# A fused hybrid-mixer and ConvFFN layer on one core: two early steps of the up stage moved, the residual loads of the down stage split up, and the last scaling shared by two engines

## What is computed

```python
h = rmsnorm(x, norm1_g)
x = x + hybrid_mixer(h, ...)          # attention and mLSTM heads, W_in and W_out
h = rmsnorm(x, norm2_g)
u = causal_dwconv(h @ w_up, w_conv, b_conv)      # w_up 1024 x 5632, three taps
gate, up = split(u, 2)
x = x + (silu(gate) * up) @ w_down               # w_down 2816 x 1024
return rmsnorm(x, final_g)
```

## Time and profile before

| | |
|---|---|
| median of 3 runs | 1053.67 us (1052.75 to 1054.21) |
| profiled execution: its own time | 1054.37 us |
| its span, first to last instruction | 1052.6 us |
| PE busy | 1024.2 us (97% of the span) |
| DVE busy | 728.0 us (69%) |
| ACT busy | 500.2 us (48%) |
| mean granted PE clock | 0.994 of full speed |
| DMA | 107.75 MB, mean 102 GB/s |
| raw<-in_w_up, 512 KB: median from issue to landing | 4.8 us |

### The profile page before, as it was taken

The page is one execution under the profiler, slowest core; times in us unless marked ns, Lnnn a source line. Parts: engine busy times, 40 slices in busy tenths (PEclk is TensorE's granted clock), DMA queues, the critical chain, the costliest instruction groups (busy, mean ns, idle before and its releaser), DMA issues.

```text
span 1052.6 us, 13256 instructions
## 1 busy us (share of the span) xinstructions
PE 1024.2 (97%) x4933; PEld 845.9 (80%) x4933; DVE 728.0 (69%) x1153; ACT 500.2 (48%) x939; POOL 74.4 (7%) x80
## 2 busy tenths in 40 slices
PE   5999999999989999799999999999999999999997
PEld 4888888888778888688888888888888887888886
DVE  5352555641675567898778777777787778996796
ACT  7632445443653324465445445454454634444564
POOL 5020222220330000000000000000000000000000
PEclk9999999999999999899999999999999999999999
DMA  7126111110242224233223122231230998125104
GB/s 223 43 73 149 40 31 30 40 41 21 62 140 81 80 80 140 60 101 115 66 81 100 60 94 88 80 100 60 81 101 21 362 391 306 59 86 186 58 1 161
DMA packets 108640, 107.75 MB, mean 102 GB/s; under 512 B 13330, under 2 KB 81032, under 8 KB 108576
## 3 DMA queue, kind: packets, MB, share of 16 engines
q1 hardware_dynamic: 107040, 103.56, 31.1%
q0 software_dynamic: 1536, 3.34, 1.3%
HBM read 86.93 MB, written 19.96 MB: 102 GB/s over the span
## 4 chain that ended last, share of the span: by engine, by line
PE 91%; DVE 4%; ACT 2%; DMA 2%; issue 1%; SPq 0%; DVEq 0%; POOL 0%; ACTq 0%; POOLq 0%
PE pz L1815 19%; PE pz L2112 7%; PE pz L2113 7%; PE pz L2114 7%; PE pd L2112 6%; PE pd L2114 6%; PE pd L2113 6%; PE pd L2136 4%; PE pd L2133 4%; PE pd L2135 4%; PE pd L2043 3%; PE pd L2041 3%; PE pd L2042 3%; PE pz L2133 3%; PE pz L2136 3%; PE pz L2135 3%
## 5 line engine op out<-in xcount | busy, mean ns | idle before, releaser
L1016 ACT ACTIVATE ws_hi<-raw 128x512 fp32r<-128x512 f32 x88 | 52.9, 626 | 107.8 <-PE pz L2114 52.1
L1815 PE MATMUL pz<-h_hi,w_hi 128*128 128x512 f32 x304 | 99.2, 399 | 2.6 <-DVE h_lo L1203 2.6
L2112 PE MATMUL pz<-ht_hi,ws_hi 128*128 128x512 f32 x240 | 94.7, 395 | 5.3 <-DVE u L1597 5.3
L1815 PE MATMUL pz<-h_lo,w_hi 128*128 128x512 f32 x304 | 96.8, 391 | 0.0
L1815 PE MATMUL pz<-h_hi,w_lo 128*128 128x512 f32 x304 | 96.3, 390 | 0.0
L2113 PE MATMUL pz<-ht_lo,ws_hi 128*128 128x512 f32 x240 | 94.5, 394 | 0.0
L2114 PE MATMUL pz<-ht_hi,ws_lo 128*128 128x512 f32 x240 | 94.3, 393 | 0.0
L2112 PE MATMUL pd<-ht_hi,ws_hi 128*128 128x512 f32 x200 | 77.8, 389 | 0.0
L2113 PE MATMUL pd<-ht_lo,ws_hi 128*128 128x512 f32 x200 | 77.8, 389 | 0.0
L2114 PE MATMUL pd<-ht_hi,ws_lo 128*128 128x512 f32 x200 | 77.8, 389 | 0.0
L1620 DVE SCALAR_TENSOR_TENSOR gate<-u,vec,gate 128x1023 f32<-128x1023 f32 (+1 forms) x44 | 56.5, 1284 | 20.0 <-ACT gate L1058 19.2
(11 more groups left out here) (297 smaller groups left out, 2495.7 us busy)
## 6 DMA issues: line engine op xcount, KB each, us to landing
raw<-in_w_up SPq DMA_DIRECT2D x48, 512.0 KB, 4.8
b<-in_w_down SPq DMA_DIRECT2D x49, 256.0 KB, 7.2
act_rows<-gate SPq DMA_DIRECT2D x22, 512.0 KB, 2.7
a<-act_rows SPq DMA_DIRECT2D x44, 256.0 KB, 5.4
raw<-in_w_in SPq DMA_DIRECT2D x14, 512.0 KB, 3.7
x_in<-in_x SPq DMA_DIRECT2D x8, 512.0 KB, 6.0
x_again<-in_x SPq DMA_DIRECT2D x8, 512.0 KB, 4.1
b_raw<-in_w_down SPq DMA_DIRECT2D x14, 256.0 KB, 6.3
```

The source lines that it names most:

```text
L1016: nc.scalar.activation(ws_hi[m][:, :, :], summand(p, i), ACT.Copy).then_inc(s["ws_hi_made"], 1)
L1815: ins = mm(dst[:, h * HALF:(h + 1) * HALF], w[:, c], v[:, h * HALF:(h + 1) * HALF], start=first, stop=last)
L2112: mm(dst, wh[:, k, :], xh[:, k, :], start=begins and k == 0, stop=False, skip_group_check=not begins)
```

## The change

1. **Up stage.** `add_11(0)` moves on DVE from the head of the loop over pairs to right behind `sum_low(0, 7)`; for all other pairs it stays. `keep_22(0)` moves on ACT to right behind `keep_21(0)`, ahead of `sum_high(1, 6)` and `sum_high(1, 7)`.
2. **Down stage.** SP loads only the block x_whole[0, 0] early, behind `load_a21(4)`; the two others come behind all stream and a21 loads. The first `y_add` waits for one block, the one of phase 2 for three. SP waits for nine adds instead of one before it loads x12 and the final gain.
3. **Tail.** `y_root` is split: the means are taken from the half that was squared first, all eight ahead of the last squares (`y_mean`), and the root adds the half that is squared last. For the last tile, half 0 is multiplied by the gain by DVE early (`y_gained`), and scaled by the reciprocal on ACT (`y_half_made`), while DVE scales half 1.
4. Two pairs of semaphores are made one (`gain_turned`, `gain_ready` into `vec_turned`, `vec_ready`), with counts raised by one; no instruction comes or goes by that.

```diff
             for k in range(STREAM_RING):
                 load_stream(k)
-            for k in range(3):
-                load_a21(k)
             for i in range(NT // 2):
                 sp.wait_ge(x1_stored[i], 64)
             act_ready(FT - 2)
             act_ready(FT - 1)
-            for (m, half), block_ in x_whole.items():
+
+            def load_x1(m, half):
                 rows = x1_d[m * HALF:(m + 1) * HALF, half * HALF:(half + 1) * HALF]
-                sp.dma_start(block_[:, :, :], rows.rearrange("(t p) c -> p t c", p=P)).then_inc(s["x1_loaded"], 16)
+                sp.dma_start(x_whole[m, half][:, :, :], rows.rearrange("(t p) c -> p t c", p=P))\
+                  .then_inc(s["x1_loaded"], 16)
+
+            for k in range(STREAM_RING):
+                load_a21(k)
             for k in range(STREAM_RING, KT):
                 load_stream(k)
                 load_a21(k)
+                if k == 4:
+                    load_x1(0, 0)
+            sp.wait_ge(s["x1_loaded"], 16)
+            load_x1(1, 0)
+            load_x1(1, 1)
             for k in range(6):
                 load_b21(k)
             sp.wait_ge(s["down_split"], 2 * down_step(7, 5) + 2)
-            sp.wait_ge(s["y_added"], 1)
+            sp.wait_ge(s["y_added"], 9)
             for t in range(4):
                 sp.dma_start(x_block[0, 1][t], x1_d[t * P:(t + 1) * P, HALF:]).then_inc(s["x1_loaded"], 16)
...
                 for half in range(2):
                     c = slice(half * HALF, (half + 1) * HALF)
-                    sp.wait_ge(s["y_made"], 2 * n + half + 1)
+                    if n == NT - 1 and half == 0:
+                        sp.wait_ge(s["y_half_made"], 1)
+                    else:
+                        sp.wait_ge(s["y_made"], 2 * n + half + (n < NT - 1))
                     sp.dma_start(out_d[i * P:(i + 1) * P, c], x_block[i // 4, half][i % 4])\
                       .then_inc(s["y_stored"], 16)
...
+            def y_mean(i):
+                half = i // 4
+                act.wait_ge(s["x2_squared"], (4 if half else 0) + i % 4 + 1)
+                nc.scalar.activation(ms3[:, i:i + 1], ss3[:, i, half:half + 1], ACT.Identity, bias=eps[:, :],
+                                     scale=1.0 / D).then_inc(s["x2_mean"], 1)
+
             def y_root(n, i):
-                act.wait_ge(s["x2_squared"], (8 if i >= 4 else 12) + i % 4 + 1)
-                nc.scalar.activation(ms3[:, i:i + 1], ss3[:, i, 0:1], ACT.Identity, bias=eps[:, :], scale=1.0 / D)\
-                    .then_inc(s["x2_mean"], 1)
-                act.wait_ge(s["x2_mean"], n + 1)
-                nc.scalar.activation(root[:, i:i + 1], ss3[:, i, 1:2], ACT.Sqrt, bias=ms3[:, i:i + 1], scale=1.0 / D)\
-                    .then_inc(s["x2_rooted"], 1)
+                half = 1 - i // 4
+                act.wait_ge(s["x2_squared"], (12 if half else 8) + i % 4 + 1)
+                act.wait_ge(s["x2_mean"], NT)
+                nc.scalar.activation(root[:, i:i + 1], ss3[:, i, half:half + 1], ACT.Sqrt, bias=ms3[:, i:i + 1],
+                                     scale=1.0 / D).then_inc(s["x2_rooted"], 1)
...
+                if i == 0:
+                    keep_22(i)
                 if i + 1 < FT:
...
                     silu(i - 1)
-                keep_22(i)
+                    keep_22(i)
...
+            for i in range(NT):
+                y_mean(i)
             for i in range(4, NT):
                 y_square(i, 0)
                 y_root(i - 4, i)
             for i in range(4):
                 y_square(i, 1)
                 y_root(4 + i, i)
+            act.wait_ge(s["x2_rstd"], NT)
+            act.wait_ge(s["y_gained"], 1)
+            nc.scalar.activation(x_block[0, 0][3], x_block[0, 0][3], ACT.Copy, scale=rstd[:, 3:4])\
+                .then_inc(s["y_half_made"], 1)
 
...
             sum_low(0, 7)
+            add_11(0)
             sum_add(0, 3)
             turned_low(5, 2)
...
             for i in range(FT):
-                add_11(i)
+                if i:
+                    add_11(i)
...
             def y_add(ph, t):
                 if ph == 0 and t == 0:
+                    dve.wait_ge(s["x1_loaded"], 16)
+                if ph == 2 and t == 0:
                     dve.wait_ge(s["x1_loaded"], 16 * 3)
                 if ph == len(DOWN_ORDER) - 1 and t == 0:
...
-                for half in range(2):
+                for half in range(n == NT - 1, 2):
...
             dve.wait_ge(s["final_g_loaded"], 32)
+            dve.wait_ge(s["x2_squared"], 4)
+            nc.vector.tensor_tensor(x_block[0, 0][3], x_block[0, 0][3], final_gb[0][:, :], ALU.mult)\
+                .then_inc(s["y_gained"], 1)
```

More of the change, by code:

```diff
@@ L330, in hymba_kernel @@
         bank = [pz[0][:, 0:HALF], pz[0][:, HALF:], pz[1][:, 0:HALF], pz[1][:, HALF:]] + [p[:, :] for p in pd]
-        names = """table_loaded gain_loaded gain_turned gain_ready vec_loaded vec_turned vec_ready
+        names = """table_loaded gain_loaded vec_loaded vec_turned vec_ready
             small_loaded gate_w_loaded const_made mem_made
@@ L351, in hymba_kernel @@
             down_summed down_hi_made down_split down_used down_done y_added x1_loaded final_g_loaded
-            x2_squared x2_mean x2_rooted x2_rstd y_made y_stored""".split()
+            x2_squared x2_mean x2_rooted y_gained y_half_made x2_rstd y_made y_stored""".split()
         s = {n: sem(n) for n in names}
@@ L743, in h_high @@
                 if n == 0:
-                    act.wait_ge(s["gain_ready"], 1)
+                    act.wait_ge(s["vec_ready"], 1)
                 act.wait_ge(s["x_turned"], n + 1)
@@ L773, in z_keep @@
                 j = b - 1
-                act.wait_ge(s["vec_ready"], 1)
+                act.wait_ge(s["vec_ready"], 2)
                 if j == MO:
@@ L1180, in after @@
                 dve.wait_ge(s["dve_step"], steps[0])
-            dve.wait_ge(s["gain_turned"], 1)
-            nc.vector.tensor_copy(vec[:, 0:NK], bank[7][:, 0:NK]).then_inc(s["gain_ready"], 1)
+            dve.wait_ge(s["vec_turned"], 1)
+            nc.vector.tensor_copy(vec[:, 0:NK], bank[7][:, 0:NK]).then_inc(s["vec_ready"], 1)
             def spread_gates():
@@ L1217, in vectors @@
             def vectors():
-                dve.wait_ge(s["vec_turned"], 3)
+                dve.wait_ge(s["vec_turned"], 4)
                 nc.vector.tensor_copy(vec[:, NK:VEC_A], bank[4][:, NK:VEC_A])
@@ L1783, in _ @@
             pe.wait_ge(s["gain_loaded"], 16)
-            nc.tensor.transpose(bank[7][:, 0:NK], vec_rows[0:NK, 0, :], ident[0:NK, 0:NK]).then_inc(s["gain_turned"], 1)
+            nc.tensor.transpose(bank[7][:, 0:NK], vec_rows[0:NK, 0, :], ident[0:NK, 0:NK]).then_inc(s["vec_turned"], 1)
             def turn_x(i, features):
@@ L1789, in turn_x @@
                     if i == 0 and k == NK - 1:
-                        pe.wait_ge(s["gain_ready"], 1)
+                        pe.wait_ge(s["vec_ready"], 1)
                     if i == NT // 2 and k >= 6:
```

## The result

| | before | changed |
|---|---|---|
| median, first series | 1053.21 us (4 runs, 1052.18 to 1054.21) | 1047.33 us (4 runs, 1046.44 to 1048.49) |
| median, second series | 1052.74 us (9 runs) | 1046.51 us (5 runs, 1046.49 to 1047.77) |
| profiled execution, own time | 1054.37 us | 1046.44 us |
| its span | 1052.6 us | 1044.7 us |

The ratio is 0.9945 (0.9933 to 0.9957) in the first series and 0.9945 (0.9931 to 0.9958) in the second: faster by 5.8 us. The forecast was 1047.1.

A forecast was written before the change was run, and what follows sets the result against it. TensorE, busy 97% of the span, was taken as the bound, with gains in its waits, low clock and tail. Up stage 3.9, down stage 2.5 and tail 0.15 made 6.55 us; 1053.67 became 1047.1 us, range 1045.2 to 1049.6.

The forecast's parts named there:

- Product 3 starts 5.55 us earlier: Up stage, pair 0: product 3 starts at 442.2 instead of 447.78, behind a new 2.7 us hole.
- The clock, 1.65 us: Up stage: TensorE's clock falls behind the new 2.7 us hole and costs 1.65 us, bounds 0 and 3.0.
- The old price of 3.0 us: Up-stage rival: the clock costs 3.0 us behind the new hole; 5.2 us saved, 1048.5 us; 25%.
- The case in which the clock stays up, 15%: Up-stage rival: no clock loss over the new hole; saves 8.2 us, 1045.5 us; 15%.
- The sum of 6.55 us: Whole kernel: 3.9 up stage, 2.5 down stage and 0.15 tail, taken from the median of 1053.67 us.
- The down stage, 2.5 us: Down stage: moving residual blocks out of the way removes the wait and slow steps; 2.5 us, bounds 0 and 2.6.
- lands near 871, 1.3 us after ScalarE wants it: Down stage: the weight pair for step 5, behind the one block left, lands 1.3 us late for ScalarE.
- The rival on the other side: Down stage: y_add(0, 0) waits for its later-issued block and stops TensorE; slower than before, about 1056 us; 2%.
- The tail, 0.15 us: Behind the last matmul: the last tile's two scalings side by side gain 0.15 us, bounds 0 and 0.45.
- The DMA engines decide: Tail: the engines, full with the last two tiles' stores but for 0.2 us between, set the end; gain 0.15 us.
- half 0 is ready at about 1049.3 instead of 1049.45: Tail: with one scaling moved to ScalarE, the last tile's first half is ready at about 1049.3, not 1049.45.
- the end would have followed the last issue: Tail alternative: the end follows the last store's issue and comes 0.45 us earlier.

The follow-up runs named there:

- up stage alone: Kernel before with only add_11(0) and keep_22(0) moved up: 1050.14 us, ratio 0.9960.
- experiment 4: Two variants of the changed kernel: first three a21 loads ahead of SP's act_rows waits, 1047.00 us; two residual blocks instead of one behind load_a21(4), 1049.02 us.
- tail alone: Kernel before with only the tail change (means first, last half scaled on ScalarE): 1052.57 us, ratio 0.9991.
- loads alone: Kernel before with only the new order of the residual loads: 1050.21 us, ratio 0.9972.
- copy alone: Kernel before with only keep_22(0) moved up on ScalarE: 1052.96 us in a single run.
- add alone: Kernel before with only add_11(0) moved up on DVE: 1050.96 us, ratio 0.9982.
- a21 ahead: Changed kernel with the first three a21 loads put back ahead of SP's waits for act_rows: 1047.00 us, ratio to before 0.9944.
- two blocks: Changed kernel with two residual blocks instead of one behind load_a21(4): 1049.02 us, ratio to before 0.9962.
- add_22(0) up: Changed kernel with add_22(0) also moved up on DVE, right behind sum_add(1, 6): 1044.05 us, ratio to before 0.9905.
- best version: Changed kernel with add_22(0) and add_22(1) moved up on DVE and the first three a21 loads ahead of SP's waits: 1043.65 us, ratio to before 0.9909.
- experiments 3 and 5: The first: changed kernel with add_22(0) moved up on DVE, 1044.05 us. The second: changed kernel again, unchanged, 1046.51 us, and the best version, 1043.65 us.

## Why the prediction was right, and where it was not

**Product 3 starts 5.55 us earlier: right.** Measured 5.55, with a hole of 2.75 us (forecast 2.7) and add_22(0) at the forecast place. That the copy had to move too, and that the loads for pair 2 are hidden, held as well.

**The clock, 1.65 us: right in size, and not always paid.** A hole of 2.7 us stands in five profiled executions (the two of the changed kernel, the up stage alone, and the two kernels of experiment 4). Behind four of them the clock fell for 3.4 us, 1.7 us lost; behind one, the first profile of the changed kernel, it stayed up. The forecast took this size from the mixer's hole, and there the same fall costs less than half of it (0.4 to 0.8 us, see the last section). At the hole of 2.7 us half of the fall is indeed lost: in the up stage alone the product behind it takes 446.47 - 442.06 = 4.41 us instead of 2.72. The old price of 3.0 us, to which I gave 25%, was never seen with this hole. The case in which the clock stays up, 15%, was seen once in five. It is also what the Trainium skill ("TensorE: Matmul & The Clock Gate", section "Why this matters for your kernels") would have, and four of five traces disagree with it.

What I had not reckoned with is that the hole in the mixer, 1.8 us in every kernel, is as uncertain. How long the clock is at its lower level at the two holes, in us, in all twelve profiled executions:

```
kernel              at the mixer's hole    at the up stage's hole
before              low 3.4 us             5.3 us hole: low 6.8 us
tail alone          low 3.4                5.3 us hole: low 6.8
loads alone         stays up               5.3 us hole: low 6.8
copy alone          stays up               5.3 us hole: low 6.8
add alone           low 3.4                3.3 us hole: low 3.4
up stage alone      low 3.4                2.7 us hole: low 3.4
changed, 1st        low 3.4                2.7 us hole: stays up
changed, 2nd        stays up               2.7 us hole: low 3.4
a21 ahead           stays up               2.7 us hole: low 3.4
two blocks          stays up               2.7 us hole: low 3.4
add_22(0) up        low 3.4                no hole
best version        low 3.4                no hole
```

(The times count from where the clock fell. At the 5.3 us holes that was inside the hole, and 5.9 to 6.1 of the 6.8 us lay behind it; at the 3.3 us hole 0.6 of the 3.4 us lay inside.) One thing goes with the mixer's outcome without exception: the matmul behind that hole starts at 295.02 to 295.27 us in the five executions in which the clock stays up, and at 295.39 to 296.35 in the seven in which it falls. What shifts that start is not shown. So a difference of two profiles holds up to 1.7 us that no edit made. It is likely part of the spread of the changed kernel's nine runs, six of which lie between 1046.44 and 1046.74 and three between 1047.77 and 1048.49; only two of the nine have a trace, both of the lower group and with one fall each. The mean granted clock was 0.997 in all six of the lower group and 0.996, 0.996 and 0.995 in the three others. A fall of 3.4 us at half the clock is 0.0016 of such a mean, so the slower three had more time at the lower level; at which hole, or whether behind the last matmul, isn't shown.

**The sum of 6.55 us against 5.8 measured (5.9 and 6.2 by the two pairs of medians): inside what can be told.** I subtracted it from a median of three runs, 1053.67. With more runs beside it the kernel before came to 1053.2 and 1052.7. With the base at 1053.2 the same sum would have given 1046.65, between the changed kernel's two medians. That 1047.1 came within 0.6 us of both medians is in part luck: a base that was a little too high and a sum that was a little too large cancel.

**The down stage, 2.5 us: right in the sum, wrong on the way.** The wait on d_lo is gone and the steps run at 2.72 us. From step 10 on (893.86 in the old count) everything is 7.88 us earlier, of which 5.30 come from the up stage, so 2.58 were gained, all there was. The step that failed is "lands near 871, 1.3 us after ScalarE wants it". That was 862.7 and three times 2.8 us, for two steps and the block, as if the loads followed one another without a break at 378 GB/s. They don't: the pair of step 5 is issued at 858.91 and 859.27, when the pair three steps earlier has been split, and lands 8.3 us later, 3.1 us late. In these 8.3 us the engines moved about 2.9 MB, which at 378 GB/s takes 7.7 us. So by this estimate the low rate around the block's load (273 to 281 GB/s) accounts for some 0.6 of the 1.8 us by which the forecast missed. The rest fits with where the pair stands: it is issued only then, and the 2.9 MB are more than the 1.6 MB of block and pair, since the loads around them move in the same time. No run moved the pair's issue alone. PE's timeline says what was left of the slack:

```profile
872.38 0.39 PE L2164 MATMUL pz<-d_hi,d_hi 128*128 128x512 f32 x1
```

That is the first matmul of step 5; its last low part, made at 869.47 on DVE (0.68 us), was there at 870.15. So 2.2 us were left, and DVE's four adds, which follow at 3.0 us a step (870.67, 873.67, 876.68, 879.69), took 1.2 of them, and 1.0 was left. The term came out whole because the slack took up the error, and the edge was nearer than I wrote. Why the rate is low there is open. The later a21 loads are not the reason, since in experiment 4 they came sooner and the rates were lower still (227 to 259 GB/s, at shares of 0.65 to 0.83, so the engines were idle for part of that time). Whether the block's own form (128x4x512, from a DRAM buffer) is slower to move wasn't tried.

**The rival on the other side**, y_add waiting for its block: nowhere. DVE's longest wait there is for ACT's d_hi (3.33 us at 868.25), and the first add runs at 870.67, in its place.

**The tail, 0.15 us: mis-sized, under 0.1 measured.** "The DMA engines decide" held: in windows of 0.1 us they finish 5.3 to 5.4 us after the last add's start in both kernels, and the span ends 6.21 us after it where it was 6.23. The step that failed is "half 0 is ready at about 1049.3 instead of 1049.45": I took ACT's scaling for about 0.6 us, the row of it says 0.72, and so half 0's store starts 0.04 us sooner instead of 0.15. The windows of the changed kernel show what is left to the end:

```profile
1040.90:1042.20 1.30, 0.00 (x0) 0.00 (x0) 0.67 (x1) 0.64 (x1) 0.00 (x0) 0.71 1.01 375
1042.20:1042.40 0.20, 0.00 (x0) 0.00 (x0) 0.00 (x0) 0.00 (x0) 0.00 (x0) 0.50 0.55 185
1042.40:1043.90 1.50, 0.00 (x0) 0.00 (x0) 0.00 (x0) 0.00 (x0) 0.00 (x0) 0.50 0.93 350
```

As in rows 10, there are two full stretches with 0.2 us between them: tile 2's stores, then tile 3's 524 KB from 0.8 us after the first issue (0.9 before). That the second half's store is issued 0.3 us sooner is hidden behind the first half's bytes. The Trainium skill ("DMA: Bandwidth & Descriptors", section "Anatomy of one DMA") prices each transfer by itself, with some 2 us of fixed cost and a share for its bytes. It gives this for transfers issued by POOL, while these are SP's. By that sum the end would have followed the last issue, 0.45 us as forecast and 0.32 us as the rows have it; no run shows that.

## What to carry to other kernels

When a queue's order is changed to close a wait, follow the same chain on to the next consumer of that engine: here that gave the new hole to 0.05 us, and moving its add too (one more line of the order) was worth about half as much again as the whole change. One half of such a move can be worth nothing alone, so cost them together. Where a profile holds short holes of TensorE, read the clock behind each of them in both profiles before a difference is put down to an edit. And price a load from the moment at which its own wait lets it be issued, and not as one of a row without gaps: by the estimate above that was two thirds of the error here, and a rate from another stretch (378 GB/s for 273 to 281) one third.

## What the runs showed of the hardware

- At the same hole (1.8 us, the same instructions around it) the granted clock fell for 3.4 us in seven of twelve profiled executions and stayed up in five; at the hole of 2.7 us it fell in four of five.
- Every fall at a hole of 1.8 to 3.3 us lasted 3.4 us, whatever the hole's length. At the 5.3 us hole it lasted 6.8 us in all four executions, and there the clock had fallen inside the hole.
- A fall in the mixer is not paid in full: between the changed kernel's two profiles, the one without it gained 1.60 - 1.17 = 0.43 us between the mixer's hole and product 3, not 1.7, and over the other kernels with the same program ahead of that product the difference is up to 0.8 us. In all five executions without it PE has two waits there that the others lack or have shorter (on ml_p 0.7 us, on nothing the profile shows 0.6 instead of 0.2), so other work is likely to set part of that pace.
- ACT's scaling of 128x512 from SBUF by a column took 0.72 us beside DVE's scaling in all profiles read for it (the changed kernel, the tail alone, experiments 3 and 5), where its copies of 128x512 elsewhere take 0.57 to 0.63. Which of the two, the column or DVE beside it, makes the difference isn't shown.
